# Linear attention on one NeuronCore: the next head's preparation is dealt beside the second half of the scan's steps instead of all of them

## The chip, the cores and the metric

The kernel runs on one NeuronCore of a Trainium2 chip. The metric is the time of one execution on the device, in microseconds (us), as the median of several runs.

## The reference, cut to what matters

The program is a two-layer first block (four mixers and a gated feed-forward) followed by a second block: gated linear attention (GLA), then a mixture of experts. The change touches only the four GLA heads of the second block. For each head there is a forward and a backward scan over chunks of 64 positions: first over 4 context chunks, of which only the state is kept, then over the 8 chunks of the sequence, with outputs.

```python
def step(s, inp):                       # one chunk, one head
    qc, kc, vc, gc = inp
    cum = jnp.cumsum(gc, axis=2)        # gc: log decays of the chunk
    last = cum[:, :, -1:, :]
    s_new = exp(last)[..., None] * s + einsum('bhjd,bhje->bhde', kc * exp(last - cum), vc)
    if not with_outputs:                # context chunks
        return s_new, None
    scores = einsum('bhid,bhjd,bhijd->bhij', qc, kc, decay)     # inside the chunk
    o = einsum('bhid,bhde->bhie', qc * exp(cum), s) + einsum('bhij,bhje->bhie', scores, vc)
    return s_new, o
...
logdecay = log_sigmoid(low @ w_gb + b_g) / 16       # needs the gate matmul per head and direction
o = o * rsqrt(mean(o * o)) * norm_g                 # per head, then times silu(r) and w_out
```

Sizes: 512 positions, 256 context positions, 4 heads with 128 key and 256 value columns.

## The kernel before, in words

A core has five engines, each with a program of its own: PE (matrix products), DVE (vector), ACT (activations and copies), POOL and SP (DMA issue). Each works its program off in order and waits at semaphores.

`gla_heads` (L2838) holds the stage. It has three streams: `scan` (the heads themselves, `gla_scan_stream`, 17 steps per head), `prep` (what a head needs before its scan, `gla_prepare_stream`, 7 steps per head) and `modulation` (sums for a later stage, one small step per head and one at the end). The function builds a list `plan` of stream numbers. PE, ACT and DVE all walk the same list: for each entry the engine appends what that stream does on this engine in its next step (`run`). The plan thus fixes the order on three engines; it waits for nothing itself. POOL and SP have their own programs, which the plan does not order. Head 0 is prepared before its scan; beside each of the heads 0, 1 and 2 the next head is prepared; head 3 runs alone.

The 17 scan steps of a head, with the lines of their main instructions:

- Step 0: PE computes the 32 score products of the head (L2729) and the state update products of chunk step s = 0 for both directions (L2716). These wait for the preparation's transposed keys (six `k_out` copies). DVE masks the scores (L2809).
- Step 1: PE multiplies masked scores with values (L2746, 32 products).
- Steps 2 to 13 are chunk steps s = 0 to 11. PE issues the update products for s+1 (L2716) and, from s = 4, the outputs of the state of s-1 (L2762, 8 products). DVE adds the update to the decayed state, two operations per s for s = 0 to 10 (L2820, L2823). Update products for s+1 wait for the state of s-1; the output of s waits for the state of s-1; the state of s waits for the outputs of s-1, because two buffers take turns.
- Step 14: ACT squares the outputs (L2787). Step 15: PE averages them (L2772), ACT makes the inverse root `rs` (L2790, L2792). Step 16: DVE multiplies outputs, gain and gate into `y` (L2831, L2832); the next head's masks follow on DVE.

The 7 preparation steps, for the next head:

- prep 0: gate product of the forward direction on PE (L2467, four instructions), taken by ACT (L2476, L2478). prep 1: the same for the backward direction, whose product waits until ACT has emptied the same PSUM bank; then ACT's two activations that make the softplus (L2484, L2486).
- prep 2: PE transposes values (L2552, 8), ACT copies them (L2605); DVE runs the decay sums (L2491, and three scans of L2493), which wait for the softplus. prep 3: PE transposes 4 more value blocks, ACT copies (L2610); DVE centres the sums (L2501 to L2507).
- prep 4: ACT takes the exponentials (L2511, L2515, L2516), which wait for the centred sums. prep 5: DVE scales keys (L2524) as soon as the first exponential is there, then queries and step factors (L2528 to L2535). prep 6: PE transposes the keys (L2552, 12; the last four wait for the first two copies, since they share a bank) and ACT copies them in six pieces (L2627, `k_out`).

One POOL task matters: during head 0 it clears the second set of key buffers (L2703, six memsets). These buffers lie on key and query columns still in use, so it waits for all scaled keys of head 1; the first `k_out` copy of head 1 waits for all six memsets.

`alternate(17, 7)` deals one preparation step after the scan steps 2, 4, 7, 9, 12, 14 and 16, that is after chunk steps s = 0, 2, 5, 7, 10, after the squares and at the end.

Of the kernel before, what the change touches and what calls it, by code (L numbers as in the profile page):

```python
# [47 lines left out]
GLA_H = 4  # L48
# [536 lines left out]
def run(engine, streams, plan):  # L585

    programs = [s[engine]() for s in streams]
    for i in plan:
        next(programs[i])
    for p in programs:  # L590
        for _ in p:
            raise ValueError("the plan ends before the stream")
# [874 lines left out]
def alternate(first, second):  # L1467

    plan, done = [], 0
    for i in range(first):  # L1470
        plan.append(0)
        upto = (i + 1) * second // first
        plan += [1] * (upto - done)
        done = upto
    return plan
# [1362 lines left out]
def gla_heads(c, w, gates, pr, sums, fill, filled, w_out, swept):  # L2838

    nc = c.nc  # L2840
    sn = {n: c.sem(f"gla_sn_{n}") for n in ("zeroed", "scored", "masked", "update", "added", "e_scaled", "summed", "squared",
                                            "ms", "rs", "ended")}
    mod = ModRows(c, "b2_mod", sums, lambda j: sums.sums[0][1][j][:, 0:S], lambda j: c.ps[:, 0, :], c.ps[:, 0, :])
    prep = gla_prepare_stream(c, w, gates, pr, sn, mod.copied)
    scan = gla_scan_stream(c, w, pr, sn, fill, filled, w_out)

    def sum_parts():
        for j in range(sums.count):
            mod.sum_quarter(j)
            yield  # L2850
        mod.turn(nc.tensor)
        yield

    def copy_parts():
        for j in range(sums.count):
            mod.copy_quarter(nc.scalar, j)
            yield
        yield

    def add_bias():  # L2860
        for j in range(sums.count):
            yield
        mod.add_bias(nc.vector)
        yield

    modulation = dict(pe=sum_parts, dve=add_bias, act=copy_parts)
    streams = [scan, prep, modulation]
    plan = [1] * prep["steps"]
    for h in range(GLA_H):
        steps = alternate(scan["steps"], prep["steps"]) if h + 1 < GLA_H else [0] * scan["steps"]  # L2870
        at = steps.index(0) + 1
        plan += steps[:at] + [2] + steps[at:]
    plan[-3:-3] = [2]
    with nc.Block() as block:
        @block.sync
        def _(sp):
            scan["sp"]()
            mod.spread(sp)

        @block.gpsimd  # L2880
        def _(pool):
            c.sweep(pool, swept)
            scan["pool"]()

        @block.tensor
        def _(pe):
            run("pe", streams, plan)

        @block.scalar
        def _(act):  # L2890
            act.preload_act_table_set(LN_EXP)
            run("act", streams, plan)

        @block.vector
        def _(dve):
            run("dve", streams, plan)
# [582 lines left out]
def block_two_mixer(c, ahead, swept, held, first_sums, gla_out):  # L3479
    nc, dram = c.nc, c.dram  # L3480
    w = Gla(c)
    tables = c.k[:, K_AT["m_ld"]:K_AT["m_ld"] + 6 * S]
    acc = [c.k[:, K_AT["cos"]:K_AT["cos"] + D], *(tables[:, i * D:(i + 1) * D] for i in range(3))]
    free = c.p[:, w.v:w.v + 8, :].rearrange("p a n -> p (a n)")
    rest = AdaLN(c, "b2_mod", L, 2, 4, [free[:, i * D:(i + 1) * D] for i in range(4)], [(c.cond[:, :], acc)])
    pr = {n: c.sem(f"gla_pr_{n}") for n in ("z", "z_in", "exp", "soft", "gate", "exps", "k_done", "q_done", "steps", "v_turn",
                                            "v_out", "k_turn", "k_out", "chain")}
    gates = GlaGates(c, w, pr)
    gla_project(c, w, gates, ahead, rest, first_sums, swept)
    held.close()  # L3490
    filled = c.sem("slots_filled")
    rows_of = dram["slot_out"].rearrange("(q a) (b n) -> q (a b) n", q=Experts.MAX_BLOCKS * P // S, n=S)
    fill = [(rows_of[q, :, :], dram["xT"].rearrange("k p n -> (k p) n"))
            for q in range(Experts.MIN_BLOCKS * P // S, Experts.MAX_BLOCKS * P // S)]
    gla_heads(c, w, gates, pr, rest, fill, filled, gla_out, [*ahead.loaded, ahead.high, ahead.low, c.tables_in])
# [260 lines left out]
```

## Time and profile before

| | us |
|---|---|
| median of 3 runs | 2551.28 |
| the three runs | 2546.16, 2551.28, 2555.0 |
| the profiled execution | 2546.32 |
| span of its trace | 2544.3 |
| TensorE's mean granted clock in it | 0.962 of full |

The GLA heads take from about 1938 us to 2098 us of the span. The profile's chain of waits follows the work back from the last instruction, and its pieces lie in the expert stage behind them; for the heads one reads the timeline of each engine. In a timeline row stand the start, the duration, the engine, the line, the operation, output and inputs, and how many like instructions are merged; in brackets how long the engine was idle before it and what ended that idle time. PSUM tiles are `ps`; the names of SBUF tiles are those of reused storage (`ring`, `w2b`, `h`, `p`, `y`). The head that a line belongs to is known by its time.

### The profile page before, as it was taken

To read this page: it belongs to the slowest core of one execution; us is meant where nothing else is said; L and a number is where in the kernel's file an instruction comes from. 1 tells how busy PE (TensorE), PEld (TensorE's weight loads), DVE (VectorE), ACT (ScalarE), POOL (GpSimd) and SP (SyncE) were. 2 spreads that over 40 slices of the span, in tenths; PEclk is the share of its full clock that TensorE was granted. 3 is DMA by queue.
4 is the path that set the end of the run, shared out by engine and by line. 5 is a ranking of instruction groups with operands and counts; after the bars stand their busy time and mean duration, and the time that the engine had idled before them with its cause. 6 is when DMAs were issued, how large, how long until landed. Compare 5 with 4: busy or idle time off the path is not lost. (4 is left out here: it accounts for less than half of the span.)

```text
span 2544.3 us, 31895 instructions
## 1 busy us (share of the span) xinstructions
PE 2274.3 (89%) x11349; PEld 1813.1 (71%) x11349; DVE 1599.0 (63%) x2267; ACT 1074.0 (42%) x1628; POOL 175.6 (7%) x201
## 2 busy tenths in 40 slices
PE   4998689799999999878979999999998879699994
PEld 3776566678888777656757888788877666577773
DVE  6655656555567565565755555774643665699996
ACT  3444244343342234343344333423333434577774
POOL 0001100000000000101000000000000101122232
PEclk9999899999999999989999999998999999899997
DMA  7650000223225356100012322445624001899995
GB/s 297 214 174 5 1 34 1 83 76 98 91 89 194 118 179 213 47 1 1 34 50 75 99 91 95 154 152 187 211 89 165 1 1 43 311 396 393 401 397 215
DMA packets 95430, 348.29 MB, mean 137 GB/s; under 512 B 12360, under 2 KB 14520, under 8 KB 95056
## 3 DMA queue, kind: packets, MB, share of 16 engines
q1 hardware_dynamic: 88688, 323.67, 36.0%
q0 software_dynamic: 3888, 14.16, 1.5%
q10 hardware_dynamic: 2736, 8.92, 0.9%
q8 instruction: 70, 1.15, 0.2%
q14 instruction: 48, 0.39, 0.0%
HBM read 333.55 MB, written 21.54 MB: 140 GB/s over the span
## 5 line engine op out<-in xcount | busy, mean ns | idle before, releaser
L498 PE MATMUL ps<-a_hi,w_hi 128*128 128x512 f32 x1408 | 572.4, 407 | 42.6 <-DVE y_lo L1829 19.3
L500 PE MATMUL ps<-a_hi,w_lo 128*128 128x512 f32 x1408 | 564.4, 401 | 0.0
L499 PE MATMUL ps<-h_lo,w_hi 128*128 128x512 f32 x1280 | 508.1, 397 | 0.0
L462 DVE TENSOR_TENSOR w_lo<-ring,w_hi 128x1024 fp32r<-128x1024 f32 x178 | 218.1, 1225 | 384.9 <-ACT w_hi L457 384.5
L457 ACT ACTIVATE w_hi<-ring 128x1024 fp32r<-128x1024 f32 x178 | 188.3, 1058 | 531.6 <-PE ps L500 518.4
L498 PEld LDWEIGHTS ps<-a_hi,w_hi 128*128 128x128 f32 x1408 | 268.7, 191 | 116.6 <-DVE w_lo L462 28.5
L500 PEld LDWEIGHTS ps<-a_hi,w_lo 128*128 128x128 f32 x1408 | 268.2, 190 | 66.4
L499 PEld LDWEIGHTS ps<-h_lo,w_hi 128*128 128x128 f32 x1280 | 243.6, 190 | 60.8 <-issue 2.9
L3210 DVE TENSOR_TENSOR moe_w_lo<-p,moe_w_hi 128x1024 fp32r<-128x1024 f32 x187 | 245.8, 1360 | 15.0 <-ACT moe_w_hi L3309 13.7
L3309 ACT ACTIVATE moe_w_hi<-p 128x1024 fp32r<-128x1024 f32 x204 | 216.0, 1062 | 69.0 <-PE ps L3252 61.1
L2052 PE MATMUL ps<-p_lo,down_hi 128*128 128x512 f32 x352 | 137.8, 392 | 0.0
L3250 PE MATMUL ps<-moe_w_hi,moe_x_hi 128*128 128x512 f32 x272 | 111.2, 409 | 11.2 <-DVE moe_w_lo L3210 6.4
L3252 PE MATMUL ps<-moe_w_lo,moe_x_hi 128*128 128x512 f32 x272 | 107.9, 397 | 0.0
L3251 PE MATMUL ps<-moe_w_hi,moe_x_lo 128*128 128x512 f32 x272 | 107.7, 396 | 0.0
L1969 ACT ACTIVATE down_hi<-down_raw 128x1408 fp32r<-128x1408 f32 x32 | 44.1, 1379 | 144.8 <-PE ps L2053 144.8
L499 PE MATMUL ps<-y_lo,w_hi 128*128 128x512 f32 x192 | 77.3, 402 | 0.0
L2052 PEld LDWEIGHTS ps<-p_lo,down_hi 128*128 128x128 f32 x352 | 66.1, 188 | 14.4
L1904 DVE SCALAR_TENSOR_TENSOR y<-ps,cols,y 128x510 f32<-128x510 f32 x88 | 65.9, 748 | 13.5 <-DVE y L1901 5.5
L290 DVE SCALAR_TENSOR_TENSOR y<-vt,cond,y 128x1024 f32<-128x1024 f32 x56 | 70.6, 1279 | 5.2 <-DMA vt<-in_ada 5.1
L1973 DVE TENSOR_TENSOR down_lo<-down_raw,down_hi 128x1408 fp32r<-128x1408 f32 x32 | 52.0, 1624 | 33.7 <-ACT down_hi L1969 33.4
L3250 PEld LDWEIGHTS ps<-moe_w_hi,moe_x_hi 128*128 128x128 f32 x272 | 52.1, 192 | 28.1 <-POOL moe_w_lo L3210 11.1
L1874 ACT ACTIVATE y<-ps,cols 128x512 f32<-128x512 f32 x88 | 67.2, 764 | 9.4 <-PE ps L500 9.4
(635 smaller groups left out, 4185.1 us busy)
## 6 DMA issues: line engine op xcount, KB each, us to landing
ring<-in_ffn_up SPq DMA_DIRECT2D x88, 512.0 KB, 3.4
ring<-in_w_in SPq DMA_DIRECT2D x72, 512.0 KB, 5.3
p<-in_moe_gate SPq DMA_DIRECT2D x68, 512.0 KB, 6.1
p<-in_moe_up SPq DMA_DIRECT2D x68, 512.0 KB, 5.3
p<-in_moe_down SPq DMA_DIRECT2D x68, 512.0 KB, 6.2
vt<-in_ada SPq DMA_DIRECT2D x64, 512.0 KB, 3.9
p<-in_ada SPq DMA_DIRECT2D x48, 512.0 KB, 5.6
down_raw<-in_ffn_down SPq DMA_DIRECT2D x32, 704.0 KB, 5.1
```

Source lines behind the costliest of these rows:

```text
L290: ins = nc.vector.scalar_tensor_tensor(out, self.piece[b], factor, out, ALU.mult, ALU.add)
L457: self.c.nc.scalar.activation(self.c.w_hi[:, s % 2, :], self.c.slot(s), ACT.Copy).then_inc(self.high, 1)
L462: self.c.nc.vector.tensor_tensor(self.c.w_lo[:, s % 2, :], self.c.slot(s), self.c.w_hi[:, s % 2, :].bitcast(F32), ALU.subtract).then_inc(s ...
L498: nc.tensor.matmul(bank, c.w_hi[:, s % 2, at], hi(kt), start=(kt == 0), stop=False)
L499: nc.tensor.matmul(bank, c.w_hi[:, s % 2, at], lo(kt), start=False, stop=False)
L500: return nc.tensor.matmul(bank, c.w_lo[:, s % 2, at], hi(kt), start=False, stop=(kt == KT - 1))
L2052: nc.tensor.matmul(bank, down.w_hi[n % 2][:, at], c.p_lo[:, kt, :], start=False, stop=False)
L3210: ops.tensor_tensor(m.w_lo[:, n % 4, :], m.raw[n], m.w_hi[:, n % 4, :].bitcast(F32), ALU.subtract).then_inc(low[n], 1)
L3250: nc.tensor.matmul(bank, x[0], w_hi, start=start, stop=False)
L3251: nc.tensor.matmul(bank, x[1], w_hi, start=False, stop=False)
L3252: return nc.tensor.matmul(bank, x[0], w_lo, start=False, stop=stop)
L3309: nc.scalar.activation(m.w_hi[:, n % 4, :], m.raw[n], ACT.Copy).then_inc(high[n], 1)
```

## The change

Two lines in `gla_heads`. For the heads with a successor, the first 8 of the 17 scan steps are issued with no preparation step between them; the 7 preparation steps are dealt over the remaining 9.

```diff
     for h in range(GLA_H):
-        steps = alternate(scan["steps"], prep["steps"]) if h + 1 < GLA_H else [0] * scan["steps"]
+        behind = scan["steps"] // 2
+        steps = [0] * behind + alternate(scan["steps"] - behind, prep["steps"]) if h + 1 < GLA_H else [0] * scan["steps"]
         at = steps.index(0) + 1
         plan += steps[:at] + [2] + steps[at:]
```

Written out, with 0 for a scan step and 1 for a preparation step (the modulation step stays behind the first scan step):

```
before: 0 0 0 1 0 0 1 0 0 0 1 0 0 1 0 0 0 1 0 0 1 0 0 1
after:  0 0 0 0 0 0 0 0 0 0 1 0 1 0 1 0 0 1 0 1 0 1 0 1
```

The preparation steps now stand behind chunk steps s = 7, 8, 9 and 11, behind the squares, behind the inverse root and at the end. No instruction and no semaphore is added or removed, and head 3 has the order it had.

## Rows read from the trace of the kernel before

**Rows 1.** Windows: stretch, length, busy us (count) by engine, PEclk, DMA share, GB/s.
```profile
2026.60:2067.10 40.50, 33.72 (x213) 27.07 (x212) 27.01 (x50) 17.77 (x30) 2.05 (x2) 0.92 0.00 1
2050.80:2054.40 3.60, 3.53 (x13) 3.17 (x14) 3.46 (x9) 0.00 (x0) 0.00 (x0) 0.50 0.00 0
2079.00:2090.50 11.50, 11.50 (x85) 10.91 (x83) 5.56 (x12) 0.00 (x0) 0.00 (x0) 1.00 0.01 1
```

**Rows 2.** Timeline of PE, heads 0 to 2 (prepared beside): anchors and gates.
```profile
1954.11 0.60 PE L2716 MATMUL ps<-ring,y 128*128 128x256 f32 x2
...
1986.53 1.15 PE L2729 MATMUL ps<-w2b,ring 128*64 128x64 f32 x32
...
1994.09 0.60 PE L2716 MATMUL ps<-w2b,p 128*128 128x256 f32 x2
...
2026.62 1.15 PE L2729 MATMUL ps<-ring 128*64 128x64 f32 x32
...
2034.19 0.60 PE L2716 MATMUL ps<-ring,y 128*128 128x256 f32 x2
...
2035.14 1.55 PE L2467 MATMUL ps<-vt,ring 16*128 16x512 f32 x4
...
2038.55 1.55 PE L2467 MATMUL ps<-vt,ring 16*128 16x512 f32 x4
...
2050.87 1.22 PE L2716 MATMUL ps<-ring 128*128 128x256 f32 x2 [3.67 <-DVE h L2823]
```

**Rows 3.** Timeline of PE, head 3, which runs alone.
```profile
2067.14 1.15 PE L2729 MATMUL ps<-w2b,ring 128*64 128x64 f32 x32
...
2074.70 0.60 PE L2716 MATMUL ps<-w2b,p 128*128 128x256 f32 x2
...
2085.13 0.65 PE L2716 MATMUL ps<-w2b,p 128*128 128x256 f32 x2
...
2086.88 0.43 PE L2716 MATMUL ps<-w2b 128*128 128x256 f32 x1
```

**Rows 4.** Timeline of DVE beside head 2.
```profile
2044.77 1.76 DVE L2491 SCALAR_TENSOR_TENSOR h<-h 128x1536 f32<-128x1536 f32 x1 [1.33 <-ACT h L2486]
...
2050.34 1.66 DVE L2823 SCALAR_TENSOR_TENSOR h<-h,small,ps 128x256 f32<-128x256 f32 x4
2051.91 0.18 DVE L2501 COPY small<-h 128x24 f32<-128x24 f32 x1
...
2061.86 1.28 DVE L2528 SCALAR_TENSOR_TENSOR w2b<-p,w2b 128x512 f32<-128x512 f32 x2
...
2065.45 0.75 DVE L2831 SCALAR_TENSOR_TENSOR ring<-ps,cols,ring 128x512 f32<-128x512 f32 x1 [2.08 <-ACT ring L2792]
```

**Rows 5.** Timeline of ACT beside head 2.
```profile
2056.31 1.48 ACT L2511 ACTIVATE ring<-h 128x1536 f32<-128x1536 f32 x1 [0.21 <-DVE h L2507]
...
2058.74 0.21 ACT L2516 ACTIVATE small<-small 128x24 f32<-128x24 f32 x1
2061.32 1.09 ACT L2787 ACTIVATE ring<-ps 128x512 f32<-128x512 f32 x2 [2.37 <-PE ps L2762]
2063.99 0.69 ACT L2790 ACTIVATE ring<-ps,k 128x512 f32<-128x512 f32 x1 [1.59 <-PE ps L2772]
...
2065.25 0.57 ACT L2627 ACTIVATE w2b<-ps 64x512 f32<-64x512 f32 x1
```

**Rows 6.** Timelines of DVE, POOL and ACT at the end of head 0.
```profile
1979.11 0.68 DVE L2524 TENSOR_TENSOR ring<-ring,p 128x512 f32<-128x512 f32 x1
...
1980.65 0.42 DVE L2524 TENSOR_TENSOR ring<-ring,vt 128x256 f32<-128x256 f32 x1
...
1982.91 1.67 POOL L2703 MEMSET p<- 64x512 f32 x3
...
1984.62 0.59 ACT L2627 ACTIVATE w2b<-ps 64x512 f32<-64x512 f32 x1 [0.15 <-POOL p L2703]
```

**Rows 7.** Timeline of DVE, the last product of the last head.
```profile
2096.98 0.69 DVE L2832 TENSOR_TENSOR y<-w2b,p 128x512 f32<-128x512 f32 x1
```

## The prediction, before the change was run

> **What bounds the kernel now.** The chain of waits comes first, and it says little here: its pieces lie in the expert stage. What it leaves to find out is whether time lost in the attention heads reaches the end. It does: the last product of the last head [rows 7] feeds the output projection, and in the heads the DMA share is 0.00 [rows 1], so no transfer fills meanwhile that a longer stage would give more time to. I carry a head's loss to the end one to one.
>
> Then the windows by head. Beside head 2, PE is busy for 33.7 of 40.5 us and DVE for 27.0 [rows 1]: no engine is full, so order and latency decide. The timeline of PE shows where. From the first update product of chunk step 1 to the score products of the next head, a head with a preparation beside it takes 32.42 (head 0: 1986.53 - 1954.11), 32.53 (head 1: 2026.62 - 1994.09) and 32.95 us (head 2: 2067.14 - 2034.19) [rows 2, 3]. I measure between these two points, because what lies between a score product and the first update is ordered as before. Inside lies one stall: PE waits 3.67 us for a state that DVE can't compute, since it is busy with the preparation's decay sums [rows 2, 4]. After it the granted clock stands at 0.50 of full, 1.2 GHz, for the whole stretch of 3.6 us that I read [rows 1]. Last comes head 3, alone: from chunk step 4 on PE is busy for all of 11.5 us [rows 1]; a step there takes 1.75 us (2086.88 - 2085.13) [rows 3] and PE is its bound.
>
> **The change part by part.** All instructions stay, so the question is which of them stand one behind another. Preparation is one chain over three engines: gate, second gate, softplus, decay sums, centring, exponentials, scaled and transposed keys, key copies, and only then the next head's scores. Before, it began behind chunk step 0 and had nearly the whole head to run in. Now it begins behind step 7.
>
> *Removed.* The first eight steps run as in head 3: the slot behind step 7 comes 10.43 us after the first update (2085.13 - 2074.70) [rows 3]. The stall of 3.67 us in mid-head and the low clock behind it go. On PE nothing else is saved, since its gates and transposes only move.
>
> *The chain from there.* Gate to gate: PE needs 1.55 for the gate and 1.75 for a chunk step between, 3.30 us; the two gates now stand 3.41 apart (2038.55 - 2035.14) with ACT's emptying of the bank between them, so that wait adds 0.1 at most [rows 2, 3]. Second gate to the decay sums: 2044.77 - 2038.55 = 6.22 [rows 2, 4]; it is ACT's emptying and softplus, and DVE waits for it now too (its 1.33 of idle time). Decay sums: 2050.34 - 2044.77 = 5.57 [rows 4].
>
> Here is the new stall. DVE has the sums in its program ahead of the state of step 10. PE, after the second gate, has one more chunk step (1.75), the transposes and the outputs of step 10, some 3.5 us with the gate itself 5, before it wants that state for step 11; the state comes 6.22 + 5.57 = 11.8 us after the second gate began. PE stands for about 7 us where it stood for 3.67. And where work of later chunk steps covered the rest of the chain before, nothing is left to cover it:
>
> - The state of step 10: half of the four operations between 2050.34 and 2051.91, 0.79 [rows 4].
> - Centring: 2051.91 to the first exponential at 2056.31, 4.40 [rows 4, 5].
> - Exponentials: 2056.31 to 2058.95 (2058.74 + 0.21), 2.64 [rows 5]. They now stand ahead of the inverse root in ACT's program. The squares fit in ahead of them, beside the centring. The mean on PE is ready 2.67 after the squares (2063.99 - 2061.32) [rows 5], about when the exponentials end, so it is hidden; without them as cover it would set the root.
> - Root to the first key copy: 2065.25 - 2063.99 = 1.26 [rows 5].
> - First key copy to the next head's scores: 2067.14 - 2065.25 = 1.89 [rows 3, 5].
>
> The sum is 10.43 + 3.30 + 6.22 + 5.57 + 0.79 + 4.40 + 2.64 + 1.26 + 1.89 = 36.50 us. Against 32.42, 32.53 and 32.95 that is +4.1, +4.0 and +3.5: 11.6 us.
>
> *Head 0 pays once more.* POOL clears the second key buffers only when all scaled keys of head 1 exist, and the first key copy waits for that. Now this is hidden behind the root almost wholly (0.15 left) [rows 6]. From the last key product to the first copy it takes 1984.62 - 1980.65 = 3.97, and the last key product starts 1.54 after the first (1980.65 - 1979.11) [rows 6]. The first product can start when the first exponential ends (1.48) [rows 5]: 1.48 + 1.54 + 3.97 = 7.0 after the exponentials begin. By way of the root the copy would start after 2.64 + 1.26 = 3.9. So +3.1.
>
> *DVE at the end of a head.* The products for `y` now stand directly behind the query products. They begin some 1.48 + 1.95 + 1.5 = 4.9 us after the exponentials, with 1.95 for the keys (1.54 and 0.42) and 1.5 from 2061.86 on as an estimate for the rest; the scores follow after 5.8 [rows 4 to 6]. That is 0.9 ahead of the scores; before it was 1.7 (2067.14 - 2065.45) [rows 3, 4]. So the next head's masks come up to 0.8 later. What hides this is PE's own work ahead of the masked products; I take 0.2 for each of the heads 1 and 2, near the lower end, 0.5 in all, with 0 and 1.6 as ends.
>
> Total: 11.6 + 3.1 + 0.5 = **+15.2 us**. Against the profiled execution (2546.3) this gives 2561.5. That execution lies at the lower end of the three runs (2546.2 to 2555.0); the new time will be a median of runs, so I set the sum on their median: 2551.3 + 15.2 = **2566 us**, 0.6% slower.
>
> **The rivals.**
>
> *The low clock lasts.* The new stall is twice as long and lies at the end, where PE has little to do between the mean, the transposes and the scores. The granted clock was at 0.50 behind the old stall [rows 1], and two update products that take 0.65 in head 3 took 1.22 there [rows 2, 3]. If it stays low into the next head, the stretch from the scores to the first update (2074.70 - 2067.14 = 7.56 us) [rows 3] grows. Its ends are 0 and a doubling, 7.56; much of it is waiting for copies and masks, so I take half: 3.8 a head, 11 in all, 2577 us. Against it speaks the mean of head 2's window, 0.92: at half of full that is (1 - 0.92) x 40.5 / 0.5 = 6.5 us in the whole head, so behind the old stall the clock came back soon [rows 1]. The Trainium skill ("TensorE: Matmul & The Clock Gate", Part 1) says that the throttled state is the default and activity releases it; by that rule a quiet tail behind a long stall keeps the clock low, which is this rival, and the sum would be its time. No row of before shows a stall followed by so quiet a stretch. Chance 0.14.
>
> *Faster: the chain is covered after all.* If softplus, sums and centring were done by the time DVE turns to step 10, PE alone would bound the head: the chunk steps of head 3 to their end (2090.5 - 2074.7, about 16 us), the moved PE work (two gates of 1.55, transposes of some 1.4) and the present end from the squares to the scores, 2067.14 - 2061.32 = 5.8 [rows 2, 3, 5], together some 26.3. That would be 6 us less than now per head, -19 in all: 2532. For it speaks that PE is the full engine in the second half [rows 1] and the old stall goes. It decides at one point: the stretch from the second gate to the state of step 10 must not exceed the 5 us that PE still has to do there. The rows say 11.8 [rows 2, 4]. Chance 0.03.
>
> *About the same.* The chain is as described, but shorter where its links were measured beside other work: the memsets overlap with the root as they do now, and each head loses 1 to 2 us instead of 4. Then +3 to +6: 2554 to 2557. For it: beside PE's and DVE's other work, engines wait for semaphores that the chain would no longer share. Against it: DVE's part, 5.57 + 4.40, runs without a gap now. Chance 0.09.
>
> **How the numbers follow.** A measurement of this kernel can tell about 0.3%, 7.7 us, from no change. My forecast (+15, chance 0.74) and the low clock (0.14) are slower by more: 0.88. Within 0.3% is the third rival: 0.09. Faster: 0.03. The forecast's own bounds are 11.6, if the memsets were hidden and the masks cost nothing, and 16.3; with the spread of the runs of before (some 5 us below the median) its time may be as low as 2558. The low clock takes the upper end to 2577, of which I leave the last part out. Range 2557 to 2575.
>
> **What the profile would show.** Heads 0 to 2 longer from score products to score products, head 0 by some 7 us and the others by 4; head 3 unchanged. In each of the three, no PE stall in the first half, and one of about 7 us ahead of the outputs of step 11, released by DVE. ACT's exponentials between squares and root. For head 0, the first key copy idle some 3 us behind POOL's memset. A head of 26 us with a gap-free PE, or a clock still at 0.50 at the next head's masked products, would show a rival right; a stretch from second gate to state 10 much under 11 us would make the prediction wrong.

## The result and the profile after

The changed kernel takes 2568.14 us (median of 5 runs, 2566.69 to 2571.24) against 2551.28 us before (also five runs by then, three of which the table above shows): a ratio of 1.0067, with a 95% interval from 1.005 to 1.0085. That is 16.9 us slower; the prediction was 2566 us, 15.2 slower.

The two traces differ in their spans by 20.5 us (2564.8 - 2544.3). 2.4 of it lie ahead of the heads, where no instruction was moved: the first scores begin at 1943.15 instead of 1940.78. This start varies from trace to trace (1940.8 to 1953.1 in the kernels of this study, whose work up to there is the same), so for the rest of this text the heads are measured by themselves, each kernel in one profiled execution, from the first score products to the start of the last product for `y`: 156.2 us before, 174.97 after, **+18.8**. From there to the end of the span the two are alike (447.3 and 446.7 us), as the prediction assumed when it carried the heads' loss to the end.

By head, from scores to scores, and inside it from the first update product of chunk step 1 to the next scores:

| head | before, scores to scores | after | before, first update to scores | after | predicted |
|---|---|---|---|---|---|
| 0 | 45.75 | 54.45 | 32.42 | 40.27 | 39.6 |
| 1 | 40.09 | 46.19 | 32.53 | 37.03 | 36.5 |
| 2 | 40.52 | 44.48 | 32.95 | 36.92 | 36.5 |

The timeline of PE in the changed kernel, head 1 and into head 2. Columns as in the rows of before: start, duration, engine, line, operation, output and inputs, count; in brackets the idle time before it and what ended it.

```profile
2006.76 0.60 PE L2716 MATMUL ps<-w2b,p 128*128 128x256 f32 x2
...
2017.28 1.55 PE L2467 MATMUL ps<-vt,ring 16*128 16x512 f32 x4
...
2020.66 1.55 PE L2467 MATMUL ps<-vt,ring 16*128 16x512 f32 x4
...
2024.83 1.00 PE L2762 MATMUL ps<-w2b,h 128*128 128x64 f32 x8
2032.99 1.97 PE L2762 MATMUL ps<-w2b,h 128*128 128x64 f32 x8 [7.16 <-DVE h L2823]
2034.75 1.06 PE L2552 MATMUL ps<-k,vt 128*128 128x128 f32 x4
2037.05 3.55 PE L2772 MATMUL ps<-w2b,k 128*128 128x512 f32 x4 [1.24 <-ACT w2b L2787]
...
2043.23 0.63 PE L2552 MATMUL ps<-k,ring 128*128 128x128 f32 x4 [1.73 <-ACT y L2627]
2043.79 1.15 PE L2729 MATMUL ps<-ring 128*64 128x64 f32 x32
```

The stall of 3.67 us in the middle of the head is gone [rows 2]; one of 7.16 us stands ahead of the outputs of step 11, released by DVE's state. Between the first update and that stall the timeline shows no idle time of PE. DVE and ACT show why the state came so late, and what follows it:

```profile
2026.88 1.76 DVE L2491 SCALAR_TENSOR_TENSOR h<-h 128x1536 f32<-128x1536 f32 x1 [5.58 <-ACT h L2486]
2028.68 3.74 DVE L2493 TENSOR_TENSOR_SCAN h<-k,h 128x512 f32<-128x512 f32 x3
2032.45 0.88 DVE L2823 SCALAR_TENSOR_TENSOR h<-h,small,ps 128x256 f32<-128x256 f32 x2
2033.24 0.18 DVE L2501 COPY small<-h 128x24 f32<-128x24 f32 x1
...
2039.16 0.69 DVE L2524 TENSOR_TENSOR ring<-ring,p 128x512 f32<-128x512 f32 x1 [1.55 <-ACT ring L2511]
```

```profile
2036.39 1.09 ACT L2787 ACTIVATE w2b<-ps 128x512 f32<-128x512 f32 x2
2037.64 1.48 ACT L2511 ACTIVATE ring<-h 128x1536 f32<-128x1536 f32 x1 [0.16 <-DVE h L2507]
...
2040.07 0.21 ACT L2516 ACTIVATE small<-small 128x24 f32<-128x24 f32 x1
2040.64 0.69 ACT L2790 ACTIVATE w2b<-ps,k 128x512 f32<-128x512 f32 x1 [0.36 <-PE ps L2772]
...
2041.90 0.57 ACT L2627 ACTIVATE ring<-ps 64x512 f32<-64x512 f32 x1
```

Link by link, from the first update (2006.76): gate after 10.52 (10.43 predicted), second gate 3.38 (3.30), sums 6.22 (6.22), state of step 10 after 5.57 (5.57), centring from 0.79 on (0.79), exponentials 4.40 (4.40), their end 2.64 (2.64), then 0.36 of waiting that was not in the sum, root to key copies 1.26 (1.26), scores 1.89 (1.89). DVE waits 5.58 us with the state of step 10 queued behind its sums; before it waited 1.33 [rows 4].

At the end of head 0 POOL and ACT show the other term:

```profile
1991.80 1.68 POOL L2703 MEMSET w2b<- 64x512 f32 x3 [44.80 <-issue]
1993.53 1.67 POOL L2703 MEMSET p<- 64x512 f32 x3
```

```profile
1995.23 0.59 ACT L2627 ACTIVATE w2b<-ps 64x512 f32<-64x512 f32 x1 [2.45 <-POOL p L2703]
```

The first key copy of head 1 waited 0.15 us for the memsets before [rows 6]; now ACT stands idle for 2.45 us until they are done.

The windows hold what the timeline only hints at, the clock (stretch, length, busy us and count of PE, PE's loads, DVE, ACT, POOL, then granted clock, DMA share, GB/s):

```profile
1996.50:2003.00 6.50, 6.41 (x44) 3.98 (x44) 2.44 (x6) 2.33 (x4) 2.04 (x2) 0.52 0.00 0
2033.00:2037.00 4.00, 2.81 (x12) 2.41 (x12) 3.83 (x7) 1.15 (x4) 0.00 (x0) 0.50 0.00 0
2037.00:2040.40 3.40, 3.35 (x4) 1.36 (x5) 1.85 (x4) 3.12 (x5) 0.00 (x0) 0.52 0.00 0
```

Behind the stall the clock is at 0.50 of full, 1.2 GHz, and stays there through the mean (3.55 us instead of 1.98 at full clock). After head 0, which ends with one more wait, it is low until well into head 1: the scores take 1.98 us instead of 1.15, and the stretch from the scores to the first update 9.16 instead of 7.56.

### The profile page after: what moved, and what is told of

Its sections match the earlier page's. It is cut to its first block and busy times, and to the rows that moved or that the text cites. A ratio compares the mean times of both kernels' runs of the same rounds, so it can differ in the third digit from the quotient of the medians.

```text
span 2564.8 us, 31895 instructions
## 1 busy us (share of the span) xinstructions
PE 2282.2 (89%) x11349; PEld 1817.6 (71%) x11349; DVE 1597.4 (62%) x2267; ACT 1073.4 (42%) x1628; POOL 176.5 (7%) x201
```

## The experiments

Theory A says that the preparation is one chain over PE, ACT and DVE, that the change starts it late, and that its uncovered length sets the head. Theory B, in several forms, puts the loss elsewhere: in PE's stall, in the sums' place, in the crowding at the end. Theory C is the low clock. Theory D, in the last experiment only, is that PE's own work and the low clock at a head's end set the head. All times of the heads below are from one trace of each kernel; the medians of whole runs, which carry the varying start, stand in a table behind the experiments.

**The stall alone.** On DVE only, the state of chunk step 10 goes ahead of the sums:

```diff
+        own = list(steps)
+        if h + 1 < GLA_H:
+            third = [i for i, x in enumerate(own) if x][2]
+            own[third:third + 2] = own[third + 1], own[third]
+        dve_plan += own[:at] + [2] + own[at:]
...
-            run("dve", streams, plan)
+            run("dve", streams, dve_plan)
```

> The changed kernel, but on DVE alone the state of chunk step 10 stands ahead of the preparation's decay sums (L2491, L2493); PE and ACT keep the changed order. DVE has 5.6 us of idle time there, waiting for the softplus, so the state costs it nothing. Theory A (the chain from the second gate over softplus, sums, centring and exponentials to the key copies sets the head): PE's stall of 7.2 us ahead of the outputs of step 11 goes, but the chain loses only the 0.8 us of the two state operations per head; some of that may go to a lower clock in a longer quiet tail. 2564 to 2570 us, within 4 us of the changed kernel. Theory B (PE's stall itself is the loss): 7 us per head come back, 2547 us or less.

The heads take 172.4 us, 2.5 less than the changed kernel. PE in head 1:

```profile
2021.88 1.90 PE L2762 MATMUL ps<-w2b,h 128*128 128x64 f32 x16
2024.43 0.66 PE L2552 MATMUL ps<-k,vt 128*128 128x128 f32 x4 [0.66 <-ACT ring L2605]
2026.33 3.78 PE L2772 MATMUL ps<-w2b,k 128*128 128x512 f32 x4 [1.24 <-ACT w2b L2787]
2036.25 1.96 PE L2552 MATMUL ps<-k,ring 128*128 128x128 f32 x8 [6.14 <-DVE ring L2524]
```

The outputs of steps 10 and 11 run on without a stall, all 16. The idle time has only moved: PE now waits 6.14 us for the scaled keys. From first update to scores it is 36.21 instead of 37.03. The state's 0.79 us are out of the chain; that the total falls by just about as much is chance, for two smaller things nearly cancel: the root no longer waits 0.36 for the mean, but from the first key copy to the scores it takes 2.35 (2040.02 - 2037.67) instead of 1.89, with the key transposes at half clock. The 7 us of Theory B did not come back: PE's stall was a symptom.

**The memsets.** Five of six no longer wait for head 1's keys:

```diff
-                eng.wait_ge(pr["k_done"], 8)
+                eng.wait_ge(pr["k_done"], 4)
                 eng.wait_ge(pr["q_done"], 2)
                 for odd, r in enumerate((slice(64, 128), slice(0, 64))):
-                    for x in w.k_tok[1][odd]:
+                    for i, x in enumerate(w.k_tok[1][odd]):
+                        if odd == 1 and i == 2:
+                            eng.wait_ge(pr["k_done"], 8)
                         chain(eng.memset(x[r, :], 0.0))
```

> The changed kernel, with five of POOL's six memsets of the second key buffers (L2703) right after head 0's own keys are done; only the one that lies on head 1's keys still waits for them. Theory A (the first key copy of head 1 waits behind the six memsets, some 2.5 us beyond the inverse root, and the long wait also leaves PE at half clock into head 1): the 2.45 us of idle time ahead of the first key copy go, and some of the 0.8 us of slower scores and 1.6 us of slower start of head 1 with them. 3 to 5 us less than the changed kernel, 2563 to 2565 us. Theory B (the memsets are hidden by the root anyway): no change, 2568 us.

The heads take 169.99 us, 5.0 less. Head 0 falls from 40.27 to 37.26 between first update and scores, that is by 3.0, and head 1's start from 9.16 to 7.56: without the long wait at the end of head 0 the scores run at full clock again. The remaining 0.4 is no gain from the edit: head 0's start, which varies, is 0.7 shorter, and heads 1 and 2 are 0.3 longer. POOL has one memset left at the end of head 0, ACT's first key copy no longer waits for it, and the scores take 1.15 us. (In this kernel the lines from POOL's program on stand two lower.)

```profile
1996.69 0.52 POOL L2705 MEMSET p<- 64x512 f32 x1 [41.21 <-DVE ring L2524]
```

```profile
1997.58 0.57 ACT L2627 ACTIVATE w2b<-ps 64x512 f32<-64x512 f32 x1
```

```profile
1999.48 1.15 PE L2731 MATMUL ps<-w2b,ring 128*64 128x64 f32 x32
```

The median of whole runs (2567.8) does not show these 5 us; by it alone Theory B, with 2568, would stand. In this trace the start of the heads lies 5.6 us later than in the changed kernel's; where it lay in the other runs isn't known. So the gain is shown for the heads, not for the whole run.

**The chain's beginning.** Only the two gates and the softplus go back to where they were, behind chunk steps 0 and 2:

```diff
+        if h + 1 < GLA_H:
+            for _ in range(2):
+                steps.remove(1)
+            steps[5:5] = [1]
+            steps[3:3] = [1]
```

> The changed kernel, but the first two preparation steps (gates, their emptying, softplus) stand where they stood before the change, behind chunk steps 0 and 2; the other five stay late. Theory A (what costs is that the chain begins late: its head, two gates and softplus, 9.5 us, became exposed): the sums start right behind the state of step 9, 4 us earlier than in the changed kernel in each head; heads 0 to 2 from first update to scores some 32.5 us plus head 0's memsets. About 12 us less than the changed kernel, 2554 to 2557 us. Theory B (the sums and the centring so close to the head's end are what costs, wherever the chain begins): no more than 2 us less, 2566 us.

The heads take 163.4 us, 11.6 less than the changed kernel. From first update to scores it is 36.35 (head 0, with the memsets), 32.62 and 32.70, where 32.5 was expected. The stall of PE shrinks to 3.11 us, and the sums follow the state of step 9 without waiting:

```profile
2020.53 0.93 DVE L2823 SCALAR_TENSOR_TENSOR h<-h,small,ps 128x256 f32<-128x256 f32 x2 [0.83 <-PE ps L2762]
2021.37 1.75 DVE L2491 SCALAR_TENSOR_TENSOR h<-h 128x1536 f32<-128x1536 f32 x1
```

With the sums, the centring and the exponentials in the same slots as in the changed kernel, over three fifths of the loss are gone (11.6 of 18.8; without head 0's start, 10.9 of 17.9). So it is the late beginning of the chain that costs most. Of the 7.2 us that are left, 3.9 lie in head 0 between first update and scores, where the memsets stand, and 3.2 in the starts of heads 1 to 3. In heads 2 and 3 PE now waits there for DVE's masks, which come behind the products for `y`:

```profile
2042.56 3.84 PE L2746 MATMUL ps<-ring 128*128 128x128 f32 x32 [0.81 <-DVE ring L2809]
```

The whole run, 2558.5 us, has a ratio of 1.0014 to before (1.000 to 1.0029).

**A smaller dose.** A quarter of the steps alone instead of half:

```diff
-        behind = scan["steps"] // 2
+        behind = scan["steps"] // 4
```

> The first 4 scan steps instead of the first 8 are left alone (a quarter instead of half); the first gate then stands behind chunk step 3. Theory A (each head lasts as long as the slot of the first gate plus the chain behind it, where the chain is not covered): from first update to scores 35.2 us per head, 2.3 more than before, with the memsets nearly hidden (0.3 us). Some 7 us more than before, 2558 us, that is about half of the full change. Theory B (only the last quarter's crowding costs, as exponentials now stand between squares and root): no loss, 2551 us, since the exponentials stand ahead of the squares here as before.

The heads take 168.1 us, 11.9 more than before; 7 were expected. From first update to scores it is 36.58 in each of the three heads, not 35.2. ACT and PE show where the missing 1.4 us are:

```profile
2027.44 0.21 ACT L2516 ACTIVATE small<-small 128x24 f32<-128x24 f32 x1
2027.56 1.06 ACT L2787 ACTIVATE w2b<-ps 128x512 f32<-128x512 f32 x2
2032.00 0.69 ACT L2790 ACTIVATE w2b<-ps,k 128x512 f32<-128x512 f32 x1 [3.38 <-PE ps L2772]
```

```profile
2019.58 1.22 PE L2716 MATMUL ps<-w2b 128*128 128x256 f32 x2 [4.54 <-DVE h L2823]
...
2028.18 3.78 PE L2772 MATMUL ps<-w2b,k 128*128 128x512 f32 x4 [0.77 <-ACT w2b L2787]
```

Here the exponentials stand ahead of the squares, so the mean is a link of the chain, and it runs at half clock: 3.78 us against 1.98, 1.8 us more. In the changed kernel the mean lies beside the exponentials and the low clock there costs the chain at most 0.6 us a head. Theory B, no loss, falls here. What the clock costs depends on what is on the chain.

**Filling that stall.** The same kernel with 38 transposes that nothing reads, on PE ahead of chunk step 9:

```diff
+                if s == 9 and h + 1 < GLA_H:
+                    eng.wait_ge(pr["v_out"], 4 * h + 6)
+                    for _ in range(38):
+                        eng.transpose(c.ps[:, 1, 0:P], c.const("ident"), c.const("ident"))
```

> The kernel with the first four scan steps alone, with 38 transposes of a constant on PE (4.2 us of unused work) in its stall of 4.5 us ahead of chunk step 9. Without them a head took 36.6 us from first update to scores where 35.2 was expected, and the mean behind the squares 3.8 us. If the low clock behind the stall makes the difference, the mean takes 2.0 us, the outputs of the last steps half as long, and the head 33.5 to 35.2 us. If the clock doesn't matter, 36.6 us stay.

36.58 us stayed, to within a hundredth, in this one run. The fill did its work where it stood: the clock is at 1.00 in it and in the outputs behind. But step 11 still waits for the state behind the centring, 2.59 us, and the squares for the exponentials; when the mean comes, the clock has fallen again and the mean takes 3.78 us. Windows of the fill, of the last outputs and of the mean:

```profile
2022.60:2027.00 4.40, 4.31 (x40) 4.08 (x39) 4.26 (x5) 0.00 (x0) 0.00 (x0) 1.00 0.02 4
2033.10:2034.20 1.10, 1.07 (x8) 0.97 (x8) 0.37 (x1) 1.10 (x2) 0.00 (x0) 1.00 0.00 0
2035.80:2039.70 3.90, 3.81 (x6) 1.64 (x7) 1.83 (x7) 0.52 (x2) 0.00 (x0) 0.50 0.00 0
```

So my expectation was wrong in what the fill would do, not in what the half clock costs: the mean ran at half clock in both kernels. That a mean at full clock would give 34.8 us (36.58 - 1.80) is worked out, not shown.

**Filling the changed kernel's stall**, with 60 such transposes ahead of step 11:

```diff
+                if s == STEPS - 1 and h + 1 < GLA_H:
+                    eng.wait_ge(sn["added"], ADDS * h + 20)
+                    for _ in range(60):
+                        eng.transpose(c.ps[:, 5, 2 * P:3 * P], c.const("ident"), c.const("ident"))
```

> The changed kernel with 60 transposes of a constant on PE (6.6 us of unused work per head, into a free part of PSUM) in the place where PE stands 7.2 us ahead of the outputs of step 11 in heads 0 to 2. They fit into the stall. They tell what the low clock behind the stall costs. Theory A (the chain over ACT and DVE sets the head, and the clock only its fringe): the mean takes 2.0 instead of 3.4 to 3.8 us, so the inverse root no longer waits for it (0.6, 0.4 and 0.3 us), and head 0's last transposes, the scores and the start of head 1 gain up to 3 us: from the first scores to the last product for y 170 to 173.5 us instead of 175.0. Theory C (half clock in the tail is most of the 19 us): 165 us or less.

174.6 us against 175.0: nothing, less than either theory gave. Without head 0's start, which is 0.75 shorter here, the heads are even 0.4 longer than in the changed kernel. PE in head 1 (outputs now on L2766, the mean on L2776), then windows of the mean and of the stretch behind it:

```profile
2036.78 1.98 PE L2776 MATMUL ps<-w2b,k 128*128 128x512 f32 x4 [1.24 <-ACT w2b L2791]
2040.99 1.96 PE L2552 MATMUL ps<-k,ring 128*128 128x128 f32 x8 [2.23 <-DVE ring L2524]
2043.75 1.09 PE L2552 MATMUL ps<-k,ring 128*128 128x128 f32 x4 [0.79 <-ACT y L2627]
2044.77 1.98 PE L2729 MATMUL ps<-ring 128*64 128x64 f32 x32
```

```profile
2036.70:2038.80 2.10, 1.98 (x4) 0.68 (x4) 1.87 (x2) 0.68 (x3) 0.00 (x0) 1.00 0.00 0
2040.90:2047.70 6.80, 5.91 (x47) 4.80 (x48) 6.25 (x14) 5.02 (x10) 0.80 (x1) 0.50 0.01 2
```

In heads 0 and 1 the mean is at full clock now, and the root no longer waits for it. But the clock falls in the quiet stretch behind the mean instead, and the key transposes (1.09 for four instead of 0.63) and the scores (1.98 instead of 1.15) pay. The low clock has moved from the mean, where the exponentials covered it, to the scores, where nothing does. In head 2 not even that: behind the same 60 transposes the mean takes 3.61 us.

```profile
2081.90 3.61 PE L2776 MATMUL ps<-ring,k 128*128 128x512 f32 x4 [1.24 <-ACT ring L2791]
```

The Trainium skill ("TensorE: Matmul & The Clock Gate", Part 1) says that activity releases the throttle and the throttled state is the default; the trace agrees, with 1.00 in and behind the 60 transposes (2024.2 to 2031.0 and 2036.7 to 2038.8 us) and 0.50 a few us later. Theory C as the main cause falls: it wanted 165 us or less, and the heads keep their time with the clock at full through the former stall. As a fringe it stands.

**Versions built from the chain.** If the chain's beginning and DVE's blocks cost, then an early chain in small pieces should win. First, gates where the kernel before has them, DVE's sums and centring dealt one operation at a time behind the states of steps 5 to 9, the exponentials behind the squares. The preparation gets a finer program on DVE, and DVE an order of its own (0 scan step, 1 preparation step):

```diff
+DVE_PARTS = 6
+BESIDE = "000100100010010000010101"
+DVE_BESIDE = "000000001010101010100010"
...
+            for part in range(DVE_PARTS):
+                if h:
+                    (gates.scan_part if part < 4 else gates.centre_part)(eng, h, part)
+                yield
```

> Gates and transposes where the kernel before has them; only DVE's sums and centring are dealt one operation at a time behind the states of steps 5 to 9 (the rest of the centring behind the state of step 10), and the exponentials stand between squares and root; the memsets stay late. Theory A: the stall of 3.7 us of the kernel before goes, stalls of at most 1.1 us remain, scores to scores 38 us, head 0 some 3 us more for the memsets: 4 to 7 us less than before, 2544 to 2547 us. Theory B (DVE's work costs the same wherever it stands): 2551 us or more.

From first update to scores heads 1 and 2 take 30.60 and 30.66 us, 1.9 and 2.3 less than before, and the stall of 3.67 us is gone. Head 0 has 33.86, with the memsets late. But the next heads' starts take 8.96, 8.02 and 9.09 instead of 7.56, each behind a tail in which PE waits up to 2.79 us for the scaled keys, and scores and updates begin at half clock. In all 157.7 us, 1.5 more than before (0.9 of it in head 0's start, which varies), where 4 to 7 less were expected; ratio 1.0002 (0.9991 to 1.0012). The links in the middle got shorter as Theory A says; what that gave was taken back by the memsets in head 0 and by the slower starts.

Then the same with the first gate behind the masked products, the second behind chunk step 1, and the memsets early:

```diff
-BESIDE = "000100100010010000010101"
+BESIDE = "001001000100100000010101"
```

> A kernel built from the chain. The next head's first gate stands behind the masked products, the second behind chunk step 1; DVE runs the four decay sum operations and the first two of the centring one at a time behind the states of steps 5 to 9, the rest behind the state of step 10; exponentials between squares and root; five memsets early as above. Theory A (a head is the longer of PE's work and the chain from its first gate): no stall of PE above 1.5 us before the squares, scores to scores about 37 us instead of 40.1 and 40.5, some 9 us less than before in all, 2542 us. Theory B (the sums cost DVE the same wherever they stand): as before, 2551 us.

150.25 us, 6.0 less than before, where 9 were expected; the run takes 2545.97 us against 2550.49, a ratio of 0.9984 (0.9974 to 0.9994). This is the fastest kernel here, by a small margin: 0.16% against the kernel before. Its two edits were not run apart; of the 7.4 us against the kernel above, 4.6 come in head 0, where the memsets had stood, 1.2 and 0.6 in heads 1 and 2, and 1.1 in head 3's start. Heads 1 and 2 take 38.39 and 38.10 us from scores to scores, not 37. DVE works without a gap from the softplus to the end of the centring, and PE waits for it and then runs at half clock:

```profile
2054.02 0.96 DVE L2518 TENSOR_SCALAR h<-h 128x1536 f32<-128x1536 f32 x1
2056.53 0.69 DVE L2548 TENSOR_TENSOR ring<-ring,p 128x512 f32<-128x512 f32 x1 [1.55 <-ACT ring L2535]
```

```profile
2057.36 1.97 PE L2581 MATMUL ps<-k,ring 128*128 128x128 f32 x8 [2.79 <-DVE ring L2548]
2060.12 1.09 PE L2581 MATMUL ps<-k,ring 128*128 128x128 f32 x4 [0.79 <-ACT p L2656]
2061.14 1.98 PE L2754 MATMUL ps<-w2b,ring 128*64 128x64 f32 x32
```

Last, the gates as early as they go, behind the scores and behind the masked products:

```diff
-BESIDE = "001001000100100000010101"
-DVE_BESIDE = "000000001010101010100010"
+BESIDE = "010100001001000000010101"
+DVE_BESIDE = "000000010101010100100010"
```

> The chain a step further: the first gate directly behind the head's scores and the modulation's sum, the second behind the masked products, so that the softplus is there 3.4 us earlier than in e6_fine; DVE's sums and centring one at a time behind the states of steps 4 to 8, the rest of the centring behind the state of step 10. Theory A (DVE works without a gap from the softplus to the key products, so the head ends as much earlier as the softplus comes): scores to scores some 2 us less than the 38.1 to 38.4 of e6_fine, 35.5 to 36.5 us; 4 to 6 us less than e6_fine, 2540 to 2543 us. Theory D (PE's work and the low clock in the quiet tail now set the head): no more than 1 us per head, 2544 to 2546 us.

157.9 us, 7.7 more than the kernel above; the ratio to before is 0.9999 (0.9985 to 1.0014). From the gate behind the masked products to the next scores a head takes 27.5 us (2080.99 - 2053.45) against 29.7 (2061.14 - 2031.43) in the kernel above, 2.2 less, near the 2 that were expected. But from the scores to that gate it takes 13.2 us (2053.45 - 2040.26) against 8.4 (2031.43 - 2023.04):

```profile
2040.26 1.98 PE L2754 MATMUL ps<-ring 128*64 128x64 f32 x32
...
2046.60 1.52 PE L2467 MATMUL ps<-vt,ring 16*128 16x512 f32 x4 [0.79 <-ACT k L1689]
2048.06 5.47 PE L2771 MATMUL ps<-ring 128*128 128x128 f32 x32
2053.45 1.55 PE L2467 MATMUL ps<-vt,ring 16*128 16x512 f32 x4
```

The first gate with its wait for the modulation's copy (they share a bank) is 2.3 us of it; most of the rest is low clock (granted 0.59 from 2040.2 to 2046.5 us, 0.68 in the masked products), with masked products that take 5.47 us where they took 3.84. Theory A's gain did not come, and the loss, 2.1 and 2.6 us in heads 1 and 2, is more than the 1 us that Theory D allowed. In kind it is what Theory D says: past a point an earlier chain pushes PE's own work.

| kernel | heads in the trace, us | whole runs, median us | ratio to before (95%) |
|---|---|---|---|
| before | 156.2 | 2551.28 | |
| the change | 174.97 | 2568.14 | 1.005 to 1.0085 |
| state of step 10 first on DVE | 172.4 | 2566.32 | 1.0041 to 1.0076 |
| memsets early | 169.99 | 2567.77 | 1.004 to 1.0074 |
| gates early | 163.4 | 2558.49 | 1.000 to 1.0029 |
| four steps alone | 168.1 | 2563.63 | 1.0031 to 1.0064 |
| four steps alone, stall filled | 168.8 | 2568.25 (one run) | none |
| the change, stall filled | 174.6 | 2571.54 | 1.007 to 1.0106 |
| DVE in pieces | 157.7 | 2549.53 | 0.9991 to 1.0012 |
| DVE in pieces, gates and memsets earlier | 150.25 | 2545.97 | 0.9974 to 0.9994 |
| gates as early as they go | 157.9 | 2550.72 | 0.9985 to 1.0014 |

Each ratio is to the runs of the kernel before that were taken with that kernel (their medians lie between 2550.2 and 2551.3). Against these, the medians of whole runs give each difference of the heads to within 3 us, the single run of the filled kernel with four steps alone apart; so differences of 2 or 3 us between two of these kernels rest on one trace each.

## Why the prediction was right

**The chain** (11.6 us predicted): shown. Every link came within 0.1 us of its row of before, except 0.36 and 0.25 us of waiting for the mean in heads 1 and 2. It made 4.5 and 4.0 us in those heads (4.0 and 3.5 predicted). Moving its beginning back took 11.6 us off the heads (10.9 without head 0's start); taking away PE's stall alone took off 2.5.

**The new stall** of about 7 us: 7.15, 7.16 and 7.16 us, in the place and by the releaser predicted. That it is not itself the loss was implied by the sum, which counts only the chain through the state, and is shown by the first experiment.

**The memsets** (3.1 us): shown. From the first exponential to the first key copy of head 1 it took 7.03 us (1995.23 - 1988.20), where 7.0 was predicted. Moving them took 3.0 off head 0, but that this is so near 3.1 is partly luck: the copy came only 2.5 us sooner, since the root's wait for the mean (0.59) then shows, and 0.5 is the last transposes back at full clock. That clock is what the prediction left out: behind the wait at the end of head 0 it stayed low into head 1, 0.5 us at the last transposes and 1.6 us up to the first update.

**DVE at the end of the head** (0.5 us): wrong in size; in the changed kernel it cost nothing. The heads behind head 1 and 2 start in 7.56 and 7.57 us, as before, so PE's own work covers the masks. With the gates early it did cost: 0.8 us in each of heads 2 and 3.

**The low clock** was a rival of 11 us, with a chance of 0.14. As the main effect it didn't come. As a fringe it did: the 0.6 us at the means of heads 1 and 2 and the 2.1 us about head 0's end, 2.7 together. The first of these is a term that the prediction set to nothing: it had the root ready 2.67 us after the squares, from a mean at full clock, and it took 4.25 (2040.64 - 2036.39). The sum of 15.2 needs this, less 0.5 for the masks, some 0.5 for gates that stood 0.17 us later in each head, and 0.85 in head 0's start, ahead of any moved instruction, to come to the 18.8 measured. That last part is no effect of the change: the traces of this study show 13.3 to 14.2 us for the same order there.

**Faster, and about the same**, the other two rivals: the first needed the state of step 10 ready 5 us after the second gate; it came 11.8 us after it (2032.45 - 2020.66), as the rows had said. The second needed links that shrink when they stand alone; none did.

**The base.** The sum was set on the median of the runs, 2551.3, not on the profiled execution; the runs after lie about 2568, 2 us above the forecast, within what the start of the heads varies by. That whole runs came this near is partly luck: in the traces the heads lost 17.9 us without head 0's start, 2.7 more than the sum.

## What to carry to other kernels

When work for the next round is dealt beside this round, its position among the steps matters less than its chain: write out the links from its first instruction to the first user, take each link's time from rows, and compare with the work that is left behind the starting slot. A stall that appears on the bounding engine may be only where the late chain surfaces; remove it alone, as here, and it surfaces one wait further on. What worked here, in one kernel together, was to start the chain earlier, to take POOL's memsets out of its end and to cut the blocks of the engine that both streams share into pieces that fit between its urgent operations, as long as this didn't displace the other stream's own work.

## What had not been expected of the hardware

Keeping PE busy with unused work didn't buy back the clock of a later quiet stretch. With 60 transposes in the stall the clock stood at 1.00 through the mean in heads 0 and 1 and, in head 1, at 0.50 in the window that begins 2 us behind it; in head 2, with the same order of instructions, it fell in the mean already (3.61 us); with 38 it stood at 1.00 in the last outputs (2033.1 to 2034.2) and at 0.50 in the mean that began 1.65 us after them. The same four instructions of the mean took 1.98 us at one level and 3.78 at the other, and the kernel paid 0.4 us for that or 1.8, by whether another engine's work lay beside it.
